# Forgetting attention by pairs of heads, its forget sums spread over the partitions by DMA

## The reference

```python
c = jnp.cumsum(lf, axis=1)                 # sample: after the 512 cached rows
s = jnp.einsum('bqhd,bkhd->bhqk', q, k) * (FOX_HEAD_DIM ** -0.5)
s = s + (cq[..., :, None] - ck[..., None, :])
s = jnp.where(kpos[None, :] <= qpos[:, None], s, -jnp.inf)
p = jax.nn.softmax(s, axis=-1)
o = jnp.einsum('bhqk,bkhd->bqhd', p, v)
```

## Time and profile before

| | us |
|---|---|
| three runs, median (lowest to highest) | 2155.57 (2155.07 to 2157.61) |
| profiled execution, its own time | 2153.6 |
| profiled execution, span from first to last instruction | 2151.8 |
| PE busy / DVE busy / ACT busy / POOL busy | 2065.5 / 1254.3 / 772.7 / 268.4 |
| mean granted PE clock | 0.983 of full speed |

### The profile page before, as it was taken

How to read it: one execution, slowest core, us unless ns; L and a number is a source line. 1 busy time by engine, 2 the same in 40 slices (tenths; PEclk the granted TensorE clock), 3 DMA queues, 4 the chain that set the end, 5 groups by cost and what they waited for, 6 DMA issues and landing times.

```text
span 2151.8 us, 36157 instructions
## 1 busy us (share of the span) xinstructions
PE 2065.5 (96%) x15199; PEld 1984.3 (92%) x15199; DVE 1254.3 (58%) x1808; ACT 772.7 (36%) x1215; POOL 268.4 (12%) x333
## 2 busy tenths in 40 slices
PE   6899999999999989999999988988999999999999
PEld 6899999999999979668889977988999999999999
DVE  6755655556766554455555196257555556566764
ACT  4433333334333343553242243233333333333331
POOL 2000000000000430231221054200000000000000
PEclk9999999999999989999999999999999999999999
DMA  4222222236865331101011102312223222368664
GB/s 144 76 81 96 107 96 83 96 122 252 349 244 203 137 144 57 43 1 40 21 41 40 41 5 113 122 41 76 81 96 118 90 96 87 145 250 335 233 218 161
DMA packets 56289, 257.24 MB, mean 120 GB/s; under 512 B 6280, under 2 KB 10728, under 8 KB 46784
## 3 DMA queue, kind: packets, MB, share of 16 engines
q1 hardware_dynamic: 41888, 194.44, 24.7%
q0 software_dynamic: 14240, 60.49, 7.2%
HBM read 195.78 MB, written 59.12 MB: 118 GB/s over the span
## 4 chain that ended last, share of the span: by engine, by line
PE 76%; issue 11%; DVE 8%; DMA 2%; ACT 2%; POOL 1%; SPq 0%; ACTq 0%; DVEq 0%; POOLq 0%
PE ps L167 68%; PE ps L1220 2%; PE ps L1259 2%; PE ps L1232 1%; DVE sb_nrm L304 1%; POOL sb_rms L187 1%; DMA sb_h_raw<-h_kept 1%; DVE sb_x L411 1%; DVE sb_xl L452 1%; DVE sb_seg L1904 1%; DMA sb_down_raw<-wb 1%; DVE sb_xl L400 1%; DVE sb_x L438 1%; DVE sb_h_lo L885 1%; DMA sb_h_first_raw<-h_kept 1%
## 5 line engine op out<-in xcount | busy, mean ns | idle before, releaser
L167 PE MATMUL ps<-sb_xh,sb_up_hi 128*128 128x272 f32 x2480 | 719.8, 290 | 34.4 <-ACT sb_u L560 15.1
L167 PE MATMUL ps<-sb_xl,sb_up_hi 128*128 128x272 f32 x2480 | 719.2, 290 | 0.0
L167 PE MATMUL ps<-sb_xh,sb_up_lo 128*128 128x272 f32 x2480 | 716.8, 289 | 0.0
L167 PEld LDWEIGHTS ps<-sb_xh,sb_up_hi 128*128 128x128 f32 x2480 | 472.2, 190 | 37.8 <-issue 25.1
L167 PEld LDWEIGHTS ps<-sb_xh,sb_up_lo 128*128 128x128 f32 x2480 | 471.6, 190 | 0.0
L167 PEld LDWEIGHTS ps<-sb_xl,sb_up_hi 128*128 128x128 f32 x2480 | 471.3, 190 | 0.0
L167 PE MATMUL ps<-sb_h_hi,sb_down_hi 128*128 128x272 f32 x1188 | 342.2, 288 | 3.0 <-DVE sb_down_lo L830 3.0
L167 PE MATMUL ps<-sb_h_hi,sb_down_lo 128*128 128x272 f32 x1188 | 343.5, 289 | 0.0
L167 PE MATMUL ps<-sb_h_lo,sb_down_hi 128*128 128x272 f32 x1188 | 341.4, 287 | 0.0
L167 PE MATMUL ps<-sb_nh,sb_whi 128*128 128x362 f32 (+1 forms) x696 | 232.4, 334 | 6.3 <-ACT sb_fq L1067 4.4
L167 PE MATMUL ps<-sb_nl,sb_whi 128*128 128x362 f32 (+1 forms) x696 | 230.6, 331 | 0.0
(11 more groups left out here) (296 smaller groups left out, 2793.8 us busy)
## 6 DMA issues: line engine op xcount, KB each, us to landing
sb_down_raw<-wb SPq DMA_DIRECT2D x92, 704.0 KB, 5.3
sb_up_raw<-wa SPq DMA_DIRECT2D x44, 1024.0 KB, 4.8
sb_h_raw<-h_kept SPq DMA_DIRECT2D x60, 544.0 KB, 6.2
sb_wraw<-wm SPq DMA_DIRECT2D x17, 1024.0 KB, 4.8
h_kept<-sb_hs_b POOLq DMA_DIRECT2D x20, 816.0 KB, 4.8
h_kept<-sb_hbuf POOLq DMA_DIRECT2D x42, 272.0 KB, 2.3
h_kept<-sb_hs_a POOLq DMA_DIRECT2D x20, 544.0 KB, 3.2
sb_h_first_raw<-h_kept SPq DMA_DIRECT2D x10, 544.0 KB, 4.7
```

Source lines behind the costliest of these rows:

```text
L167: mm = K.nc.tensor.matmul(out, a, b, start=first and n == 0, stop=last and n == 2, skip_group_check=loose)
```

## The change: pairs of heads, and the sums by DMA

The 36 units become 18 pairs (m, j): the two heads 2m and 2m + 1, which lie on partitions 0-63 and 64-127 of fq and fk. Pairs run as (0, 8), (0, 7) ... (0, 0), (1, 0) ... (1, 8).

- scores(p) issues for each bank's worth of keys one matmul per head, with 64 partitions of queries against the same 64 partitions of keys; head s writes banks 2s and 2s + 1. The zeroed query tiles and one_head go. Each pair uses all four of these banks, so scores(p) waits for both minima of pair p - 1, and one count of s_mm covers both heads.
- values(p) issues the two heads' matmuls in turn, to partitions 0-63 and 64-127 of bank 7, and one DVE copy of 128 x 128 takes the place of two of 64 x 128. The transposes rotate over banks 4 to 6.
- The PE list is scores(it), values(it - 2), turn of both heads of pair it - 1. The orders on ACT, DVE and POOL are written to match.
- The forget sums: DVE multiplies K.cum by -8, POOL writes it to DRAM (cum_kept) and reads two heads back to all partitions with one broadcast DMA (2 x 1600 floats on 128 partitions). The next two heads come in three pieces while the loop runs: the first 384 columns into K.cb_few, columns from 512 on behind pair (0, 4), and columns below 512 behind pair (0, 0). The bias matmuls and ACT's 16 copies go.

```diff
@@ module level
-FOX_UNITS = [(h, j) for h in range(FOX_H) for j in range(NTT)]
+FOX_PAIRS = [(0, j) for j in reversed(range(NTT))] + [(1, j) for j in range(NTT)]
+FOX_UNITS = [(2 * m + s, j) for m, j in FOX_PAIRS for s in range(2)]
 PR = 4
 NU = len(FOX_UNITS)
-BIAS_AT = 4
-
-
-def bias_bank(it, q):
-
-    return 2 * ((it + 1) % 2) + q % 2 if it >= 0 else 6 + q % 2
+NFP = len(FOX_PAIRS)
+FEW = 3
+CUT = 512
@@ fox_pe, fox_act
-    def bias(h, it):
-
-        wait(e, M.smin, it)
-        for q in range(4):
-            n = 4 * h + q
-            if n == 0:
-                e.wait_ge(M.cum, 1)
-            wait(e, M.cb, n - 1)
-            nc.tensor.matmul(K.ps[:, bias_bank(it, q), :400], K.const[:, C_SEL + h * P:C_SEL + (h + 1) * P],
...
+    def scores(p):
+        m, j = FOX_PAIRS[p]
         a, r = TILES[j]
-        q = K.qz[:, u % 2, :r]
-        wait(e, M.smin, u - 1)
+        wait(e, M.smin, 2 * p)
-            parts = [(k, min(512, n - k), K.fk[:, h // 2, k:min(k + 512, n)]) for k in range(0, n, 512)]
+            parts = [(k, K.fk[:, m, k:min(k + 512, n)]) for k in range(0, n, 512)]
         else:
-            parts = [(0, PAST, K.kc[:, h // 2, :]), (PAST, TS, K.fk[:, h // 2, TP:T])]
-        for k, n, rhs in parts:
-            mm = nc.tensor.matmul(K.psf[:r, 1024 * (u % 2) + k:1024 * (u % 2) + k + n], q, rhs,
-                                  start=True, stop=True)
+            parts = [(0, K.kc[:, m, :]), (PAST, K.fk[:, m, TP:T])]
+        for k, rhs in parts:
+            n = rhs.shape[-1]
+            for s in range(2):
+                o = slice(64 * s, 64 * s + 64)
+                mm = nc.tensor.matmul(K.psf[:r, 1024 * s + k:1024 * s + k + n], K.fq[o, m, a:a + r], rhs[o],
+                                      start=True, stop=True)
         mm.then_inc(M.s_mm, 1)
...
+            wait_pt(n - 3)
+            for i, (k, w) in enumerate(tiles):
+                mm = nc.tensor.transpose(K.ps[:w, 4 + n % 3, i * P:i * P + r], K.pr[u % PR][:r, k:k + w],
+                                         K.ident[:r, :r])
...
+    def values(p):
+        m, j = FOX_PAIRS[p]
+        r = TILES[j][1]
+        e.wait_ge(M.pt_a, 2 * p + 2)
+        wait(e, M.pt_v, K.second(2 * p + 2))
+        wait(e, M.fo, p)
         tiles = [x for g in fox_groups(j) for x in g]
         for i, (k, w) in enumerate(tiles):
-            if j == NTT - 1:
-                v = K.vc[:, i, 64 * h:64 * h + 64] if i < PAST // P else K.fv[:TS, j, 64 * h:64 * h + 64]
-            else:
-                v = K.fv[:, i, 64 * h:64 * h + 64]
-            mm = nc.tensor.matmul(K.ps[o:o + 64, 6 + u % 2, :r], v, K.pt[:w, u % 2, i, :r],
-                                  start=i == 0, stop=i == len(tiles) - 1)
+            for s in range(2):
+                c = slice(64 * (2 * m + s), 64 * (2 * m + s) + 64)
+                if j == NTT - 1:
+                    v = K.vc[:, i, c] if i < PAST // P else K.fv[:TS, j, c]
+                else:
+                    v = K.fv[:, i, c]
+                mm = nc.tensor.matmul(K.ps[64 * s:64 * s + 64, 7, :r], v, K.pt[:w, s, i, :r],
+                                      start=i == 0, stop=i == len(tiles) - 1)
...
-    for it in range(NU + PR):
-        if it < NU:
+    for it in range(NFP + 2):
+        if it < NFP:
             scores(it)
-            h, j = FOX_UNITS[it]
-            if j == BIAS_AT and h + 1 < FOX_H:
-                bias(h + 1, it)
-        if 0 <= it - (PR - 1) < NU:
-            turn(it - (PR - 1))
-        if 0 <= it - PR < NU:
-            values(it - PR)
+        if it >= 2:
+            values(it - 2)
+        if 1 <= it <= NFP:
+            turn(2 * it - 2)
+            turn(2 * it - 1)
...
+    for it in range(NFP + 1):
+        if it < NFP:
+            for u in (2 * it, 2 * it + 1):
+                r = TILES[FOX_UNITS[u][1]][1]
+                n = fox_keys(FOX_UNITS[u][1])
+                e.wait_ge(M.smin, u + 1)
+                nc.scalar.activation(K.pr[u % PR][:r, :n], K.pr[u % PR][:r, :n], ACT.Exp,
+                                     bias=K.mn[:r, u % PR:u % PR + 1], scale=-1.0,
+                                     accum_out=K.rs[:r, u % PR:u % PR + 1]).then_inc(M.p_exp, 1)
+        if it:
+            turned(2 * it - 2)
+            turned(2 * it - 1)
@@ fox_small_dve
+    V.tensor_scalar(K.cum[f, :], K.cum[f, :], -8.0, None, ALU.mult).then_inc(M.cum, 1)
@@ fox_bias, fox_dve
+def fox_bias(K, e, M, u):
+    h, j = FOX_UNITS[u]
+    n = fox_keys(j)
+    c0 = 0 if j < NTT - 1 else TP
+    if h < 2:
+        e.wait_ge(M.cb, 32)
+        return K.cb[:, h % 2, c0:c0 + n]
+    if j < FEW:
+        e.wait_ge(M.cb, 48)
+        return K.cb_few[:, h % 2, c0:c0 + n]
+    e.wait_ge(M.cb, 80)
...
+    def smin(u):
+        r = TILES[FOX_UNITS[u][1]][1]
+        n = fox_keys(FOX_UNITS[u][1])
+        bias = fox_bias(K, e, M, u)
+        if u >= PR:
+            e.wait_ge(M.pt_mm, FOX_G[u - PR + 1])
+        s = K.psf[:r, 1024 * (u % 2):1024 * (u % 2) + n]
+        M.dve(V.tensor_tensor(s[:, n - r:n], s[:, n - r:n], K.mqk[:r, :r], ALU.add))
+        V.tensor_tensor_reduce(out=K.pr[u % PR][:r, :n], in0=s, in1=bias[:r],
+                               scale=-0.125, scalar=3e38, op0=ALU.add, op1=ALU.min,
+                               accum_out=K.mn[:r, u % PR:u % PR + 1]).then_inc(M.smin, 1)
+    def inverse(u):
+        r = TILES[FOX_UNITS[u][1]][1]
+        e.wait_ge(M.p_exp, u + 1)
+        wait(e, M.p_scaled, u - PR + 1)
+        V.reciprocal(K.ri[:r, u % PR:u % PR + 1], K.rs[:r, u % PR:u % PR + 1]).then_inc(M.rinv, 1)
+    def turned(u):
+        r = TILES[FOX_UNITS[u][1]][1]
+        gs = fox_groups(FOX_UNITS[u][1])
+        if len(gs) > 1:
+            n = FOX_G[u] + 1
+            e.wait_ge(M.pt_mm, n + 1)
+            wait(e, M.o_mm, u // 2)
+            m, w = len(gs[1]), gs[1][0][1]
+            V.tensor_copy(K.pt[:w, u % 2, 4:4 + m, :r],
+                          K.ps[:w, 4 + n % 3].rearrange("p (n q) -> p n q", q=P)[:, :m, :r])\
+                .then_inc(M.pt_v, 1)
+    for it in range(NFP + 2):
+        if it < NFP:
             e.wait_ge(M.s_mm, it + 1)
...
+            smin(2 * it)
+            smin(2 * it + 1)
+            inverse(2 * it)
+        if it >= 2:
+            m, j = FOX_PAIRS[it - 2]
             a, r = TILES[j]
...
+            e.wait_ge(M.o_mm, it - 1)
+            if it == 2:
                 e.wait_ge(M.kout, 16)
...
+            V.tensor_copy(K.fq[:, m, a:a + r], K.ps[:, 7, :r]).then_inc(M.fo, 1)
+        if 1 <= it <= NFP:
+            turned(2 * it - 2)
+        if it < NFP:
+            inverse(2 * it + 1)
+        if 1 <= it <= NFP:
+            turned(2 * it - 1)
@@ fox_pool
+    e.wait_ge(M.cum, 1)
+    e.dma_start(outs["cum_kept"], K.cum[SMALL_FF:SMALL_FF + FOX_H, :]).then_inc(M.cb, 16)
+    e.wait_ge(M.cb, 16)
+    e.dma_start(K.cb[:], outs["cum_kept"][0:2].partition_broadcast(P)).then_inc(M.cb, 16)
...
-        wait(e, M.s_mm, u - 1)
-        nc.gpsimd.tensor_scalar(K.qz[:, u % 2, :r], K.fq[:, h // 2, a:a + r],
-                                K.b64[:, 64 * (h % 2):64 * (h % 2) + 1], 1.0, ALU.mult, ALU.mult).then_inc(M.qz, 1)
-
-    for u in range(2):
-        one_head(u)
+    e.wait_ge(M.cb, 32)
+    e.dma_start(K.cb_few[:], outs["cum_kept"][2:4, :P * FEW].partition_broadcast(P)).then_inc(M.cb, 16)
...
+        if (h, j) == (1, CUT // P):
+            e.wait_ge(M.smin, u + 1)
+            e.wait_ge(M.cb, 48)
+            e.dma_start(K.cb[:, :, CUT:], outs["cum_kept"][2:4, CUT:].partition_broadcast(P)).then_inc(M.cb, 16)
+        if (h, j) == (1, 0):
+            e.wait_ge(M.smin, u + 1)
+            e.dma_start(K.cb[:, :, :CUT], outs["cum_kept"][2:4, :CUT].partition_broadcast(P)).then_inc(M.cb, 16)
@@ hybrid_layer, shape_constants
-        K.qz = scratch[:, :2 * P].rearrange("p (s n) -> p s n", s=2)
+        K.cb_few = scratch[:, 1024:1024 + 2 * P * FEW].rearrange("p (s n) -> p s n", s=2)
-        K.pr = [pr[:, s] for s in range(PR - 1)] + [scratch[:, 2 * P:2 * P + 1024]]
+        K.pr = [pr[:, s] for s in range(PR - 1)] + [scratch[:, :1024]]
-    for h in range(FOX_H):
-        c[SMALL_FF + h, C_SEL + h * P:C_SEL + (h + 1) * P] = -8.0
+    outs["cum_kept"] = nc.dram_tensor("cum_kept", (FOX_H, CUM), F32, kind="Internal").ap()
```

More of the change, by code:

```diff
@@ L1244, in wait_pt, with turn @@
             e.wait_ge(M.pt_v, K.second(u) + 1)
-    def values(u):
+    def turn(u):
         h, j = FOX_UNITS[u]
         r = TILES[j][1]
[L1249 to L1252, removed]
+        e.wait_ge(M.p_scaled, u + 1)
+        for g, tiles in enumerate(fox_groups(j)):
+            n = FOX_G[u] + g
+            wait_pt(n - 3)
+            for i, (k, w) in enumerate(tiles):
+                mm = nc.tensor.transpose(K.ps[:w, 4 + n % 3, i * P:i * P + r], K.pr[u % PR][:r, k:k + w],
+                                         K.ident[:r, :r])
+            mm.then_inc(M.pt_mm, 1)
+    def values(p):
[4 more added lines that the diff above has]
+        wait(e, M.fo, p)
```

(31 more changed lines are left out.)

32 lines of the change are left out of this document (1 added, 31 removed).

## The result

The changed kernel takes 2134.97 us (median of 4 runs, 2133.86 to 2136.04) against 2155.66 (four runs, 2155.07 to 2157.61), a ratio of 0.9905 with a 95% interval of 0.9892 to 0.9917. That is 20.7 us less, where 32.2 were forecast; 2135.0 lies just above the range of 2113 to 2134.

The account below looks back on a forecast made before the run. PE was taken to bound FoX, busy 108.4 of 110 us. Stage 60.5 + 5.1 + 4.5 + 4.6 = 74.7 us, ending 35.6 earlier; a clock drop adds 3.4: 2155.6 - 32.2 = 2123.4 us, range 2113 to 2134.

Parts of the forecast that it names:

- What is removed from PE: FoX on PE: array halves run together, bias matmuls go; 0.65k + 0.45 us per pair of k key tiles, 60.6 in all.
- What takes PE's place: FoX: DVE's loop sets short pairs, PE long ones; the larger of the two sums to 60.5 us over seventeen pairs.
- Handoffs: FoX: values wait for ACT's last copy of transposes; 0 to 0.7 us a pair, 0.3 taken, 5.1 us in all.
- rival 2: FoX: handoff is the bound, 0.7 us per pair, four score banks leaving no second buffer; 6.8 us more, 2130; chance 0.08.
- The clock: Start of FoX: one drop to 1.2 GHz of 6.8 us, costing half, 3.4 us; bounds none and two drops.
- rival 4: FoX: clock stays at 1.2 GHz throughout, transposes perhaps not counting as PE activity; 2166 us; chance 0.03.
- Where the stage begins: Start of FoX: without zeroed tiles PE starts at 878.3 instead of about 880.2; DVE's added multiplication costs nothing.
- The broadcasts: Forget sums by DMA, before and during FoX: hidden, taken as 0; upper bound 5 us for the first, late piece 0 to 1.
- Rival 3: FoX: the broadcast or its late piece is late, 5 us at the start and 5 at (1, 3); 2128 to 2133; chance 0.06.
- Rivals 1: FoX on PE: array halves do not run together, or only in part; 28 us back, 2151; chance 0.05.
- signs named as right: FoX: heads' scores start within some 10 ns, PE 80-85% busy, step 4 near 953 to 957, k = 1 pairs near 2.2 us.

Follow-up runs that it names:

- e1: Changed kernel with ACT's copy of the first unit's transposes moved between the two exponentials: 2125.6 us, ratio 0.9867 to the kernel before.
- e5: Changed kernel with unread identity matmuls added where PE waits in FoX, at its start and between transposes in long pairs: 2132.7 us.
- e9: Changed kernel with ACT's early copy only behind pairs of more than four key tiles, plus 17 unread matmuls at FoX's start: 2120.9 us.
- e11: As e9 without the added matmuls, so the changed kernel with only ACT's early copy behind pairs of more than four key tiles: 2123.3 us.
- e3: Changed kernel with the two heads' score and value matmuls issued one head after the other instead of alternating: 2137.8 us.
- e7: As e1, with the values of the two heads one head after the other and scores still alternating: 2133.6 us.
- e10: Changed kernel with 17 unread identity matmuls at the start of FoX and no other edit: 2132.7 us.

## Why the prediction was wrong

By its own steps:

- *What is removed from PE*: right. Row halves and column halves run together; the sum of 0.65k + 0.45 a pair gave 60.6 us, half of 13.7 us at the lower clock makes it 67.4, and the window has 68.5 busy. The rule of the Trainium skill ("TensorE: Matmul & The Clock Gate", "The mechanism"), that a weight load overlaps running matmuls only in another row group, would have left nothing to gain in the values, as the prediction read it. The trace does not agree: alternating column halves took 20.1 us, one after the other 30.5.
- *What takes PE's place*: right where it applies. The pairs (1, 1) to (1, 4) have no fourth group behind them. From their first exponential to the next pair's it took 2.6, 3.1, 3.6 and 4.0 us, which is 0.3 to 0.5 more than the larger of the two forecasts (2.25, 2.6, 3.05, 3.7), about the 0.3 taken for handoffs.
- *Handoffs*: this step failed. It said that values wait for ACT's last copy and that "the copy has the next scores beside it", 0.3 us a pair, 0.7 at most. The copy that mattered was another one: of the first unit's transposes, which frees the bank of the fourth group. The next scores do not lie beside it; they stand behind it in PE's list. The change's text showed it: `wait_pt(n - 3)`, four groups in a long pair, and ACT's order with both exponentials ahead of the copies. I had counted banks for scores (rival 2) and not for transposes. The ring is then two minima, an exponential, a copy, one to four transposes and the next scores in a row: for (0, 6) to (0, 5), 6.5 us, where the sum had 5.0 + 0.3. Eight pairs paid, seven of them 0.7 to 1.5 us and one 2.9 (against e1): 9.9 us net by e1 at the same time at the lower clock. e5 against e9, both with matmuls in the gap at the start, gives 11.1 with 3.4 us of lower clock in it. The step had 0.3 us a pair for all handoffs; this wait alone held PE for 0.8 to 4.1 us at each of the eight (13.6 in all).
- *The clock*: the kind was right and the size too small: 13.7 us at 1.2 GHz in three drops, not 6.8 in one. e9 against e11 gives 3.1 us for 6.8 us at the lower clock, so the half that I took fits as its upper end. The kernel after is 14.3 us longer in FoX than e9; the 9.9 of the wait leave 4.4 for its 13.7 us at the lower clock and the order of copies in the short pairs, about 1 more than forecast. The granted clock stayed at 1.00 through e9's FoX with its transposes in it, so rival 4's reading of them has no support here. Two of the drops follow an idle stretch that the wait itself made.
- *Where the stage begins*: 878.8, not 878.3. DVE's multiplication took 0.99 us, and in this execution the norms' sums on PE came 0.6 us later than before (their last two records start at 876.24 and 876.54, before at 875.61 and 875.91). But e9, with the same multiplication, began at 878.2, so half a microsecond is within what executions differ by, and a cost of the multiplication is not shown.
- *Outside FoX*: the span fell by 17.5 us, FoX's length by 17.6 and its start by 1.4, so what stands behind FoX took 1.4 us more. There 41.0 us pass at the lower clock, 34.1 before; that this is the 1.4 us fits by size, but nothing separates it. The medians differ by 3.2 us more than that: the profiled execution of before lay 2.0 below its median, that of after 1.1 above.
- *The broadcasts*: right, nothing waited for them.

Without most of the wait and without the drops the sum nearly stands: it put the stage from first scores to step 4 at 74.7 us, and e9, in which no drop and 5.3 us of the wait are left, needs 76.5. The stage was forecast at 78.1 with its one drop and took 90.8; the 12.7 between them are 9.9 of the wait, 1.8 that e9 still has over the sum, and 1.0 of clock and order of copies.

The rivals: rival 2 named a second buffer that is missing, and its time of 2130 was near, but by another buffer; its price of 0.7 in every pair is not what the traces show. Rival 3's 2128 to 2133 came nearer still, but nothing waited for a DMA. Rivals 1, 3 and 4 did not come. Of the signs named as right, the starts of the two heads came (6 to 7 ns) and the short pairs (2.1 to 2.3 us at one key tile); PE's busy share was 76% in place of 80 to 85, and step 4 started at 969.6 in place of 953 to 957. No sign for a held transpose had been named.

## What to carry to other kernels

When a stage is cut to half on the engine that bound it, write down for every rotating buffer how many items one iteration makes and who frees the oldest, in the order of that engine's list; a rotation that is one short puts a ring through three engines. Look then for what is queued behind the waiting instruction: here it was the next scores, and moving one copy between two exponentials gave back about half as much as the whole change had brought. A part that seems worth nothing when undone (e3) may only be hidden by another wait; undo it again once that wait is gone (e7).

## What was not expected of the hardware

- Matmuls queued one head after the other on different row halves still ran in twos, 13 ns apart (e3): at five key tiles the four passes of 512 columns started at 905.485, 905.498, 906.018 and 906.032 and the four of 128 columns behind them, so the second head's first passes ran ahead of the first head's last. Column halves do the same as long as a head has few passes: with four a head (two key tiles) the values of e3 and e7 also started in twos, 13 to 14 ns apart. With more, a head's passes ran at 0.109 us each in a row, and only the last four of the first head overlapped the first four of the second. A head's scores never have more than four passes in this kernel, so whether row halves would reach further is not shown.
- Behind three stretches with idle PE the clock fell for 3.4 or 6.8 us (in e1 once, for 13.7). Seventeen matmuls without a use, put into the gap at the start of FoX, made FoX 1.8 us shorter (e10) and 3.1 us (e9 against e11); the medians fell by 2.2 and 2.4, with overlapping intervals.
- A broadcast of 12.5 KB from DRAM to 128 partitions, 1600 KB written, landed in 9.5 us from POOL's queue, 168 KB per us, against 186 for the plain store of v (1024 KB in 5.5).
